# Softmax layers of a four-layer block: value products of a head pair ahead of the next pair's scores

## What is computed

```python
# first softmax layer (chunk_attention); chunks of 64, whole past within 8 chunks
s = einsum('bhtd,bhjd->bhtj', q / 8, k) + bias           # bias by clipped relative distance
p = softmax(where(valid, s, -1e30))
o = einsum('bhtj,bhjd->bhtd', p, v)
y = o @ w_out
# second softmax layer (odd_mixer); q and k are rms-normed, cumf is a running sum of log sigmoid
logits = einsum('bhqd,bhkd->bhqk', q, k) / 8 + cumf[q] - cumf[k]
probs = softmax(where(q >= k, logits, -inf))
o = einsum('bhqk,bhkd->bhqd', probs, v)
y = (o * silu(g)) @ w_out
```

## Time and profile before

| | us |
|---|---|
| median of three runs | 1721.59 (1721.37 to 1722.13) |
| the profiled execution | 1720.94 |
| its span | 1719.2 |
| TensorE busy | 1702.7 |
| VectorE busy | 1036.9 |
| GpSimd busy | 807.2 |
| ScalarE busy | 758.8 |

### The profile page before, as it was taken

How to read it: one execution, slowest core, us unless ns; L and a number is a source line. 1 busy time by engine, 2 the same in 40 slices (tenths; PEclk the granted TensorE clock), 3 DMA queues, 4 the chain that set the end, 5 groups by cost and what they waited for, 6 DMA issues and landing times.

```text
span 1719.2 us, 24526 instructions
## 1 busy us (share of the span) xinstructions
PE 1702.7 (99%) x9185; PEld 1427.1 (83%) x9185; DVE 1036.9 (60%) x1716; ACT 758.8 (44%) x1329; POOL 807.2 (47%) x616
## 2 busy tenths in 40 slices
PE   8999999999999999999999999999999999999999
PEld 7778788888888888888888888887888888888887
DVE  5877567555565872664475555678387845237752
ACT  4444545222222354664532222234544557666650
POOL 6635336555555473232465555553533335453342
PEclk9999999999999999999999999999999999999999
DMA  9645237444445233222274444442222123334521
GB/s 348 245 162 186 96 123 265 176 164 166 164 161 187 98 135 111 87 76 97 87 281 171 171 171 171 171 171 74 99 74 68 58 91 99 105 93 140 141 90 74
DMA packets 114829, 242.65 MB, mean 141 GB/s; under 512 B 6144, under 2 KB 27776, under 8 KB 114736
## 3 DMA queue, kind: packets, MB, share of 16 engines
q1 hardware_dynamic: 112560, 237.20, 39.9%
q10 hardware_dynamic: 2176, 4.19, 0.7%
HBM read 239.21 MB, written 2.16 MB: 140 GB/s over the span
## 4 chain that ended last, share of the span: by engine, by line
PE 90%; DMA 3%; DVE 3%; ACT 1%; POOL 1%; issue 1%; SPq 1%; POOLq 0%; DVEq 0%; ACTq 0%
PE bank L239 40%; PE bank L653 20%; PE bank L1628 5%; PE bank L1594 4%; PE bank L449 3%; PE bank L1596 2%; PE bank L428 2%; PE bank L1708 2%; PE bank L1696 2%; PE bank L1672 2%; DMA ct<-cumd 1%; PE bank L2197 1%; DMA x<-in_x 1%; PE bank L412 1%; POOL wsp L2695 1%; PE bank L1212 1%
## 5 line engine op out<-in xcount | busy, mean ns | idle before, releaser
L2695 POOL TENSOR_TENSOR wsp<-raw,wsp 128x512 fp32r<-128x512 f32 x520 | 768.1, 1509 | 814.3 <-ACT wsp L194 814.3
L239 PE MATMUL bank<-xT,wsp 128*128 128x512 f32 x2016 | 464.9, 390 | 0.0
L239 PEld LDWEIGHTS bank<-xT,wsp 128*128 128x128 f32 x2016 | 377.7, 188 | 79.9 <-issue 0.9
L194 ACT ACTIVATE wsp<-raw 128x1024 fp32r<-128x1024 f32 x132 | 139.9, 1060 | 466.8 <-PE bank L653 240.3
L653 PE MATMUL bank<-wsp,hT 128*128 128x512 f32 x1344 | 308.1, 389 | 0.0
L239 PE MATMUL bank<-wsp,xT 128*128 128x512 f32 x1248 | 298.6, 394 | 0.6 <-DVE xT L520 0.3
L653 PEld LDWEIGHTS bank<-wsp,hT 128*128 128x128 f32 x1344 | 252.3, 188 | 52.4
L239 PEld LDWEIGHTS bank<-wsp,xT 128*128 128x128 f32 x1248 | 230.6, 188 | 53.4 <-issue 5.6
L868 DVE CUSTOM_DVE_ANT_0 ada_ring<-ada_ring,crow,cols 128x1024 f32<-128x1024 f32 x96 | 148.4, 1580 | 4.8 <-DMA ada_ring<-in_ada_rows 4.7
L197 ACT ACTIVATE wsp<-raw 128x1024 fp32r<-128x1024 f32 x132 | 138.3, 1048 | 0.0
L789 DVE TENSOR_TENSOR x<-bank,x 128x512 f32<-128x512 f32 x80 | 55.2, 690 | 110.5 <-PE bank L653 110.5
(11 more groups left out here) (332 smaller groups left out, 2201.5 us busy)
## 6 DMA issues: line engine op xcount, KB each, us to landing
raw<-in_ff_w SPq DMA_DIRECT2D x64, 1024.0 KB, 5.2
ada_ring<-in_ada_rows SPq DMA_DIRECT2D x96, 512.0 KB, 6.2
tok<-in_ada_rows SPq DMA_DIRECT2D x32, 512.0 KB, 4.8
raw<-in_odd_w_in SPq DMA_DIRECT2D x16, 1024.0 KB, 5.6
raw<-in_gla_w_in SPq DMA_DIRECT2D x12, 1024.0 KB, 6.7
raw<-in_att_w_in SPq DMA_DIRECT2D x12, 1024.0 KB, 5.2
raw<-in_even_w_in SPq DMA_DIRECT2D x12, 1024.0 KB, 5.2
ring_s<-in_ada_rows SPq DMA_DIRECT2D x16, 512.0 KB, 8.0
```

The source lines that it names most:

```text
L194: act.activation(wsp[:, slot, 0, 0:HK // 2], raw[:, slot, 0:HK // 2], ACT.Copy).then_inc(hi_part, 1)
L239: mm = pe.matmul(out_ap, l, r, start=(start and a == b), stop=(stop and a == 1))
L2695: ins = pool.tensor_tensor(wsp[:, slot, 1, k], raw[:, slot, k], wsp[:, slot, 0, k].bitcast(F32), ALU.subtract)
```

## The change

In `pe_pairs`, which both softmax layers use, the loop over `times_values` of the present pair is moved ahead of the loop over `scores` of the next pair. Before, the order behind the dense products was: scores of the next pair, value products of this pair. After, it is: value products of this pair, scores of the next pair. In the last pair, which has no next one, nothing changes, and the scores of pair 0 stand ahead of the loop in both.

```diff
                 dense(u + 3)
                 if last and ahead:
                     out_ahead(1)
+                for w in range(u, u + ST):
+                    times_values(w)
                 if not last:
                     for w in range(u + ST, u + 2 * ST):
                         scores(w)
-                for w in range(u, u + ST):
-                    times_values(w)
             for t in early[2:] if ahead else early:
                 out_ahead(t)
```

## The result

The changed kernel takes **1735.65 us** (median of four runs, 1733.29 to 1736.62) against 1721.48 for the kernel before, measured again beside it (1720.74 to 1722.13). The ratio is 1.008, with a 95% interval of 1.0068 to 1.0092: slower by 14.2 us, or 0.8%. The profiled execution took 1735.19 us, its span 1733.5, which is 14.3 more than before.

The account below looks back on a forecast made before the run. TensorE, busy 99% of the span, was taken to bound the kernel. Seven stalls of 2.01 us (14.1) less 0.7 gave +13.4 on 1720.94, so 1734.3, plus 0.65 for the median: 1735.0 us; range 1733.5 to 1737.5, widened to 1730 to 1742.

Parts of the forecast that it names:

- The margin of 0.32 us: Before the change, third unit's transposes come 8.61 us behind the scores; VectorE's chain takes 8.23 plus 0.06, leaving 0.32.
- smaller stalls: Rival, chance 0.06: TensorE's modelled ends hide up to 1 us of slack; stalls of 0.6 to 1.4, +4 to +9.
- no change: Rival, chance 0.02: something other than the scores sets VectorE's start, so they come 2.33 us later for nothing; 1721.6.
- a gain: Rival, chance 0.02: scores behind value products save 0.25 us at each of 14 places, 3.5 in all; 1718.
- 2.01 us a stall: In a short pair, TensorE idles 0.91 us ahead of the first unit's transposes and 1.10 ahead of the third's.
- Seven places: Pairs 1, 2, 7 of the first layer and 1, 2, 4, 7 of the second, with short dense blocks, stall 2.01 us.
- The forecast reserve of 0.7 us: In the seven pairs with long dense blocks, cover of 9.0 us against 8.29 keeps 0.7, so they cost nothing.
- What comes back in pair 3 of the second layer: Its late-bias loss of 0.72 us was to shrink to 0 to 0.6; gain taken as 0.7, other end 0.1.
- Waits new in kind: Moved value products wait for copies of the transposed probabilities and a free output bank; both were to cost 0.
- the output bank: Ahead of the value products: bank free at 711.83, products start at 712.83, leaving 1.0 us; cost 0.
- The clock: Rival, chance 0.14: TensorE's clock falls to 1.2 GHz in the stalls, 1.55 us each; 1745.9, or 1740.5 at half.
- Seams: New neighbours, value products ahead of scores, at 14 places: taken as 0, bound 0.1 us each, 1.4 either way.

Follow-up runs that it names:

- long-only kernel: New order only in the seven places whose next pair has the long dense block, rest as in the kernel before; 1720.93 us, ratio 0.9987 to 1.0005.

## Why the prediction was right, point by point

It gave 1735.0 us with 1730 to 1742; 1735.65 was measured. The mechanism is the one forecast. But one term, 0.9 us, is missing from the sum, and that it was no larger is luck.

**The margin of 0.32 us.** Right. The chain over VectorE took 8.24 us after the change (8.23 before), and taking 0.8 out of it took 0.8 out of each stall. Both sides of the subtraction are thus shown, the cover by two experiments that gave and took 1.4 to 1.6 us of it. With 2.02 us a stall, the rivals of smaller stalls, of no change and of a gain are out. (No late bias holds up the maxima in six of the seven short pairs, not in five as the rival says: in the trace before, only pair 1 of the second layer among them waits for POOL's mask. Nothing hangs on it.)

**2.01 us a stall, in gaps of 0.91 and 1.10.** Measured 2.02, in 0.92 and 1.10. That the third unit waits for the pair's last division was shown by making it wait for its own.

**Seven places.** Right: the short ones alone give all of it, the long ones nothing that can be told from scatter. The forecast reserve of 0.7 us in the long ones is consistent with the stalls of 2.2 that they show once 2.8 to 2.9 us of cover are taken: 2.9 - 0.7 = 2.2.

**What comes back in pair 3 of the second layer.** The gap went, as forecast. The second layer starts 6.78 us later in the new trace; less these, the load is issued at 1585.73 (worked out: 1585.84) and VectorE starts at 1596.76, where the scores alone would let it at 1596.66. From issue to start it took 11.03 us (1592.51 to 1603.54) against 12.16 before; the forecast's other end kept the 12.16 and did not come. With the bias loads ahead of the panels the gap goes in the old order too.

**Waits new in kind.** Here a step was wrong. The text says that the value products wait "for two things at once", the copies of the probabilities and the output bank. There is a third, the copy of the value tiles (`v_free` in `times_values`), a wait that stands in pairs 4 to 7. In the first layer the last of these tiles are made by the very dense block that now stands directly ahead of the value products of pair 6. The rows of the kernel before would have given it: the copy ended at 783.83, 0.77 behind the 783.06 at which the products now want to start; with the 0.15 from the end of the copy to their start (787.72 to 787.87) that is the 0.9 us which it costs, shown alone by the kernel with one swapped place. The output bank was judged rightly, margin of 1.0 us behind a stall of 2.0 included: when the stall was cut to 0.6, the bank's wait appeared, with 0.40, and took back a third of the gain.

**The sum.** By the steps of the pairs the seven stalls are 1.94 to 2.08 us, 14.2 together; 0.9 for the V tiles and less 0.8 for pair 3 make 14.3, and the span grew by 14.3. The prediction's 13.4 for the profiled execution lacks the 0.9.

**The clock.** It did not fall in the changed kernel: 1.00 in both layers. The rival's mechanism is real, though: with a first gap of 2.1 us in place of 0.9 the clock fell in three of six places. The prediction's working from the rule on transposes in the Trainium skill ("TensorE: Matmul & The Clock Gate", Part 4), by which it would have fallen in all seven places of the change, is not borne out: the transposes and gaps left the clock at 1.00, 4.2 us of them in four of the places and 3.5 in the three (pair 2 of the first layer, 2 and 4 of the second) where dense work follows the 14th transpose.

**Seams.** No cost was seen in the changed kernel's order: the first layer of the long-only kernel has four new seams and takes 124.89 us against 124.92.

## What to carry to other kernels

When a step is moved past another on the busy engine, take the round trip over the other engines (here 8.3 us from the scores to the last division) and add up what the busy engine has to do in the meantime, at every iteration by itself: the same swap cost 2.0 us where the dense block ahead of the transposes was 2.9 us long and nothing where it was 5.7. Then list every semaphore that the step moved forward waits on, the ones that hold only in some iterations too; the one I left out cost 0.9 us. And a margin that is computed behind a stall goes with the stall: 1.0 us was enough behind a stall of 2.0, and became a wait of 0.4 behind one of 0.6.

## What the runs showed of the hardware

The granted clock falls to 1.2 GHz behind a recorded idle of 2.1 us in some places and not in others of the same shape. The three falls were in pairs whose 20 transposes have no dense work between them; the three that stayed have dense work behind the 14th transpose. That cannot be what decides: in slices of 0.2 us the clock reads 0.50 from 695.4, 1593.0 and 1702.4 on, at most 1.1 us behind the first transpose (694.28, 1592.59, 1702.29) and so ahead of the 14th. Up to there all six places have the same work, value products, 6 dense matmuls, scores, 6 dense matmuls and the gap. What decides stays open.

A VectorE division that reads both operands from SBUF slows down beside POOL's subtractions: 2.02 us for 128x1024 and 1.59 for 128x512, against 1.22 and 0.69 when POOL is still, or when the second operand lies in PSUM. The Trainium skill ("SBUF — State Buffer", "Who interferes with whom") has the two engines share a pair of ports which one of them holds while the other waits, and counts a VectorE operation with two SBUF inputs among those that need it. The trace agrees: the division is slower, and so are POOL's instructions beside it in the first layer (6.05 us for four, against 5.07). By how much, the page doesn't say.
